# Second layer of a two-layer transformer: the memory attention moved ahead of the differential heads, and projection units issued in halves

## The reference, cut to what matters

```python
h = rmsnorm_2(x, norm_mix[1])
proj = h @ b_w_q                       # q1 | q2 (6 heads of 64 each) | qm (4 memory heads of 64)
q1, q2 = partial_rope(rmsnorm_2(q1)), partial_rope(rmsnorm_2(q2))   # k1, k2, v come from w_kv, likewise
o = diff_attention(q1, q2, k1, k2, v, lam)     # p = softmax(q1 k1) - lam * softmax(q2 k2); o = p v
main = rmsnorm_2(o, b_subln) * (1 - lam_init)  # 6 heads of width 128
mo = memory_attention(qm, mem_n, ...)          # softmax over 256 memory rows, 4 heads
x = x + concat([main, mo]) @ w_o[1]
x = x + sqrelu_mlp(rmsnorm_2(x), w_up[1], w_down[1])
```

## Time and profile before

| | us |
|---|---|
| median of 3 runs | 1125.19 (1123.98 to 1125.64) |
| the profiled execution: its own time | 1122.91 |
| its span, first to last instruction | 1121.1 |
| TensorE matmul busy in the span | 1069.4 |
| VectorE / ScalarE / GpSimd busy | 642.4 / 546.1 / 370.1 |
| mean granted TensorE clock | 0.981 of full |

### The profile page before, as it was taken

How to read it: one execution, slowest core, us unless ns; L and a number is a source line. 1 busy time by engine, 2 the same in 40 slices (tenths; PEclk the granted TensorE clock), 3 DMA queues, 4 the chain that set the end, 5 groups by cost and what they waited for, 6 DMA issues and landing times.

```text
span 1121.1 us, 19839 instructions
## 1 busy us (share of the span) xinstructions
PE 1069.4 (95%) x8566; PEld 1047.2 (93%) x8566; DVE 642.4 (57%) x834; ACT 546.1 (49%) x770; POOL 370.1 (33%) x198
## 2 busy tenths in 40 slices
PE   6889999998999999989999999999999879999998
PEld 6889999998999999989999999999987779999998
DVE  3768855565775554727855444446765546544443
ACT  3367866633556444544344344444554544443341
POOL 2437267130555433352201342231522111252221
PEclk9999999999999999999999999999998889999999
DMA  9987648446387554534456555555532115655541
GB/s 324 285 269 243 209 151 293 159 131 203 94 282 232 188 188 166 173 113 151 135 167 198 180 187 188 186 193 171 169 128 80 39 38 188 218 174 179 182 151 39
DMA packets 173956, 197.39 MB, mean 176 GB/s; under 512 B 5379, under 2 KB 146092, under 8 KB 173740
## 3 DMA queue, kind: packets, MB, share of 16 engines
q1 hardware_dynamic: 173868, 196.11, 54.0%
HBM read 195.03 MB, written 1.06 MB: 175 GB/s over the span
## 4 chain that ended last, share of the span: by engine, by line
PE 83%; DVE 5%; ACT 4%; DMA 2%; POOL 2%; issue 2%; SPq 1%; DVEq 1%; ACTq 0%; POOLq 0%
PE bank L501 82%; DVE w_lo L1709 2%; DMA ada_raw<-in_w_ada 2%; ACT w_hi L1154 1%; SPq L457 1%; ACT ada_raw L1144 1%; POOL ada_raw L1559 1%; DMA probsT<-in_buckets 1%; PE bank L754 0%; DVE fresh L1758 0%; POOL head_bias L1594 0%; DVE big L2120 0%; ACT h_hi L1191 0%; DVE fresh L1752 0%; POOL u_lo L1527 0%
## 5 line engine op out<-in xcount | busy, mean ns | idle before, releaser
L1709 DVE TENSOR_TENSOR w_lo<-w_raw,w_hi 128x2048 fp32r<-128x2048 f32 x158 | 386.9, 2451 | 242.9 <-ACT w_hi L1154 241.6
L501 PE MATMUL bank<-h_hi,w_hi 128*128 128x256 f32 x1328 | 378.3, 290 | 11.9 <-DVE w_lo L1709 7.5
L501 PE MATMUL bank<-h_hi,w_lo 128*128 128x256 f32 x1328 | 373.6, 287 | 0.0
L1154 ACT ACTIVATE w_hi<-w_raw 128x2048 fp32r<-128x2048 f32 x158 | 301.3, 1908 | 131.4 <-PE bank L501 123.8
L501 PE MATMUL bank<-h_lo,w_hi 128*128 128x256 f32 x1328 | 347.5, 284 | 0.6 <-POOL h_lo L1527 0.6
L501 PE MATMUL bank<-u_hi,w_hi 128*128 128x256 f32 x1024 | 287.7, 285 | 4.6 <-ACT u_hi L1163 2.3
L501 PE MATMUL bank<-u_hi,w_lo 128*128 128x256 f32 x1024 | 286.5, 284 | 0.0
L1527 POOL TENSOR_TENSOR u_lo<-fresh,u_hi 128x512 fp32r<-128x512 f32 x60 | 142.3, 2374 | 411.8 <-ACT u_hi L1163 411.6
L501 PEld LDWEIGHTS bank<-h_hi,w_hi 128*128 128x128 f32 x1328 | 259.9, 196 | 17.0 <-DVE w_lo L1709 9.4
L501 PE MATMUL bank<-u_lo,w_hi 128*128 128x256 f32 x1024 | 275.5, 284 | 0.0
L501 PEld LDWEIGHTS bank<-h_hi,w_lo 128*128 128x128 f32 x1328 | 259.6, 196 | 0.0
(11 more groups left out here) (247 smaller groups left out, 1026.2 us busy)
## 6 DMA issues: line engine op xcount, KB each, us to landing
w_raw<-in_w_mlp SPq DMA_DIRECT2D x32, 1024.0 KB, 5.5
w_raw<-in_w_up SPq DMA_DIRECT2D x32, 1024.0 KB, 5.4
w_raw<-in_w_down SPq DMA_DIRECT2D x32, 1024.0 KB, 5.1
w_raw<-in_w_in SPq DMA_DIRECT2D x21, 1024.0 KB, 5.6
ada_raw<-in_w_ada SPq DMA_DIRECT2D x19, 1024.0 KB, 7.8
w_raw<-in_a_w_in SPq DMA_DIRECT2D x10, 1024.0 KB, 5.1
w_raw<-in_w_o SPq DMA_DIRECT2D x8, 1024.0 KB, 4.9
w_raw<-in_w_out SPq DMA_DIRECT2D x4, 1024.0 KB, 4.9
```

Of the source, the lines that this page charges most:

```text
L501: return pe.matmul(dst, lhsT, rhs, start=start, stop=stop, skip_group_check=True)
L1154: act.activation(w_hi[:, n % PARTS_RING, :], w_raw[:, slot_of[n], :], ACT.Copy).then_inc(hi_w, 1)
L1709: dve.tensor_tensor(w_lo[:, n % PARTS_RING, :], w_raw[:, slot_of[n], :], w_hi[:, n % PARTS_RING, :].bitcast(F32), ALU.subtract).then_inc(l ...
```

## The change: what it does

- Unit QM1 moves from sixth to second in the layer (it is unit 113 now). Its scores, turns, `m_pv`, `attended` and `to_T` stand beside units Q0, V0, K1 and Q1, ahead of the first differential head's turn. The pairs use `mem_bank` (`acc[0]`, `acc[1]` for the first, `ps_ada`, `acc[2]` for the second), and `to_T` writes `acc[3]`. New waits: `rotate("k1")` and `d_scores(0)` wait for the copies of the memory's turned probabilities.
- Units K1, Q1, K2, Q2, V1 and V2 are multiplied in halves of 24 matmuls (`half_n`; `half_tok` likewise by token tile), with attention steps between the halves; the unit's evacuation follows the second half. With `product` both output tiles of one weight row stood together.
- The memory's quarter of O1 is the first (`o_part(3, J_YM1, first=True)`), and heads 4 and 5 (quarter 2) the last.
- The programs of ScalarE, VectorE and GpSimd and the list `MISC` follow this order. The number of matmuls, transposes, splits, loads and bytes is the same.

```diff
     heads_unit("k", w["w_kv"], 0)
+    n_unit("qm1", w["b_w_q"][0], MAIN_W, "a")
     heads_unit("q", w["b_w_q"][0], 0)
     n_unit("v", w["w_kv"], MAIN_W, "a")
     heads_unit("k", w["w_kv"], 1)
     heads_unit("q", w["b_w_q"][0], 1)
-    n_unit("qm1", w["b_w_q"][0], MAIN_W, "a")
     heads_unit("k", w["w_kv"], 2)
     heads_unit("q", w["b_w_q"][0], 2)
     n_unit("v", w["w_kv"], MAIN_W + 256, "a")
...
-N_QM0, N_CONV, N_O0, N_M1K, N_MLP1, N_M1V, N_QM1, N_O1, N_MLP2 = 64, 65, 74, 78, 79, 111, 117, 122, 126
-N_K, N_Q, N_V = (112, 115, 118), (113, 116, 119), (114, 120, 121)
+N_QM0, N_CONV, N_O0, N_M1K, N_MLP1, N_M1V, N_QM1, N_O1, N_MLP2 = 64, 65, 74, 78, 79, 111, 113, 122, 126
+N_K, N_Q, N_V = (112, 116, 118), (114, 117, 119), (115, 120, 121)
...
+        mem_bank = [(acc[0], acc[1]), (ps_ada, acc[2])]
...
+                if i == 2:
+                    pe.wait_ge(turned_copied, 2 * (G_M1 + 1) + 2)
...
-            product(N_Q[0], u_hi, u_lo, job=X_MIX1, ready=(x_hi, x_lo))
+            product(N_QM1, u_hi, u_lo, job=X_MIX1, ready=(x_hi, x_lo))
...
+                else:
+                    pe.wait_ge(turned_copied, 2 * G_M1 + 2)
...
+            def half_n(n, nt, hi, lo):
+
+                if nt == 0:
+                    start_unit(n)
+                wh, wl = (t[:, n % PARTS_RING, :].rearrange("p (k n) -> p k n", k=KT) for t in (w_hi, w_lo))
+                for kt in range(KT):
+                    for i, (w, x) in enumerate(((wh, hi), (wh, lo), (wl, hi))):
+                        last = mm(lin[lin_bank[n]][:, nt * T:nt * T + T], w[:, kt, nt * P:nt * P + P], x[:, kt, :],
+                                  nt == 0 and kt == 0 and i == 0, kt == KT - 1 and i == 2)
+                if nt:
+                    last.then_inc(unit_done, 1)
...
             qk_squares("k0", N_K[0])
             rotate("k0", tiles_of("k0"))
+            product(N_Q[0], u_hi, u_lo)
+            qk_squares("qm1", N_QM1)
+            rotate("q0", tiles_of("q0"))
+            m_scores(0)
+            qk_squares("q0", N_Q[0])
             product_tok(N_V[0], h_hi, h_lo)
-            rotate("q0", tiles_of("q0"))
-            qk_squares("q0", N_Q[0])
-            product(N_K[1], h_hi, h_lo)
             spread_qk("k0", acc[3])
-            product(N_Q[1], u_hi, u_lo)
+            pe.wait_ge(rope_read, 2)
+            m_scores(1)
+            half_n(N_K[1], 0, h_hi, h_lo)
+            m_turn(0)
+            half_n(N_K[1], 1, h_hi, h_lo)
+            m_pv(0)
+            d_scores(0)
+            m_turn(1)
             qk_squares("k1", N_K[1])
+            half_n(N_Q[1], 0, u_hi, u_lo)
+            m_pv(1)
             rotate("k1", tiles_of("k1"))
-            d_scores(0)
-            product(N_QM1, u_hi, u_lo)
+            half_n(N_Q[1], 1, u_hi, u_lo)
+            pe.wait_ge(misc_read, misc_no["mem1.1"] + 1)
+            pe.wait_ge(spread_read, spread_no["qk.k0"] + 1)
+            to_T(acc[3:4], y_tok, y_turned)
+            rotate("q1", tiles_of("q1"))
             qk_squares("q1", N_Q[1])
-            rotate("q1", tiles_of("q1"))
-            spread_qk("k1", acc[3])
 
             d_turn(0)
             d_scores(1)
-            product(N_K[2], h_hi, h_lo)
+            half_n(N_K[2], 0, h_hi, h_lo)
             pv(0)
-            qk_squares("qm1", N_QM1)
+            pe.wait_ge(fresh_ready, J_YM1 + 1)
+            spread_qk("k1", acc[3])
+            half_n(N_K[2], 1, h_hi, h_lo)
 
             d_turn(1)
             d_scores(2)
-            product(N_Q[2], u_hi, u_lo)
+            half_n(N_Q[2], 0, u_hi, u_lo)
             pv(1)
             rotate("k2", tiles_of("k2"))
+            half_n(N_Q[2], 1, u_hi, u_lo)
             turn_o(0)
             qk_squares("k2", N_K[2])
 
             d_turn(2)
             d_scores(3)
-            product_tok(N_V[1], h_hi, h_lo)
-            pv(2)
+            half_tok(N_V[1], 0, h_hi, h_lo)
             rotate("q2", tiles_of("q2"))
-            spread_qk("k2", acc[3])
+            half_tok(N_V[1], 1, h_hi, h_lo)
             turn_o(1)
             qk_squares("q2", N_Q[2])
+            spread_qk("k2", acc[3])
+            pv(2)
 
             d_turn(3)
             d_scores(4)
-            pe.wait_ge(spread_read, spread_no["qk.k2"] + 1)
-            m_scores(0)
-            product_tok(N_V[2], h_hi, h_lo)
+            half_tok(N_V[2], 0, h_hi, h_lo)
             pv(3)
+            half_tok(N_V[2], 1, h_hi, h_lo)
+            turn_o(2)
 
             d_turn(4)
             d_scores(5)
-            turn_o(2)
-            m_turn(0)
-            o_part(0, J_DIFF[0], first=True)
+            o_part(3, J_YM1, first=True)
+            turn_o(3)
             pv(4)
-            m_pv(0)
-            m_scores(1)
-            turn_o(3)
+            o_part(0, J_DIFF[0])
 
             d_turn(5)
             pv(5)
             turn_o(4)
-            m_turn(1)
             o_part(1, J_DIFF[1])
-            m_pv(1)
             turn_o(5)
-            pe.wait_ge(misc_read, misc_no["mem1.1"] + 1)
-            pe.wait_ge(d_max, DIFF_HEADS)
-            to_T(acc[0:1], y_tok, y_turned)
             pe.wait_ge(fresh_hi, J_DIFF[2] + 1)
             for m in range(2):
                 part(N_O1 + m, 2, u_hi, u_lo, products="h")
-            pe.wait_ge(fresh_hi, J_YM1 + 1)
+            pe.wait_ge(fresh_lo, J_DIFF[2] + 1)
             for m in range(2):
-                part(N_O1 + m, 3, u_hi, u_lo, products="h")
-            pe.wait_ge(fresh_lo, J_YM1 + 1)
-            for m in range(2):
-                part(N_O1 + m, 2, u_hi, u_lo, products="l")
-                part(N_O1 + m, 3, u_hi, u_lo, last=True, products="l")
+                part(N_O1 + m, 2, u_hi, u_lo, last=True, products="l")
...
             split_w(N_K[0] + AHEAD)
             evac_k(0)
-            split_w(N_Q[0] + AHEAD)
+            split_w(N_QM1 + AHEAD)
             act.wait_ge(lam_dots, 1)
             act.activation(stat[:, S_LAM:S_LAM + 2], stat[:, S_DOT:S_DOT + 2], ACT.Exp).then_inc(lam_exp, 1)
+            evac_qk("qm1", N_QM1, v_tok[:, 0, :], gain=V_MQ + 1)
+            split_w(N_Q[0] + AHEAD)
             evac_q(0)
             split_w(N_V[0] + AHEAD)
+            mem_exps(0)
             evac_v_unit(0)
             split_w(N_K[1] + AHEAD)
+            mem_copy(0)
             evac_k(1)
+            mem_exps(1)
             split_w(N_Q[1] + AHEAD)
+            mem_copy(1)
+            d_exps(0)
             evac_q(1)
-            split_w(N_QM1 + AHEAD)
-            d_exps(0)
-            evac_qk("qm1", N_QM1, v_tok[:, 0, :], gain=V_MQ + 1)
-
+
+            split_w(N_K[2] + AHEAD)
             d_copy(0)
-            split_w(N_K[2] + AHEAD)
             d_exps(1)
             evac_k(2)
 
             d_copy(1)
+            o_square(0)
             split_w(N_Q[2] + AHEAD)
-            o_square(0)
             d_exps(2)
             evac_q(2)
 
             d_copy(2)
+            o_square(1)
+            split_h(J_YM1, u_hi, 6)
             split_w(N_V[1] + AHEAD)
-            o_square(1)
             d_exps(3)
             evac_v_unit(1)
 
             d_copy(3)
+            o_square(2)
             split_w(N_V[2] + AHEAD)
-            o_square(2)
             split_h(J_DIFF[0], u_hi, 0)
             d_exps(4)
-            mem_exps(0)
+            o_square(3)
             evac_v_unit(2)
 
             d_copy(4)
-            o_square(3)
-            copy_turned("mem1.", 0, G_M1, 512, mem_pT)
+            split_w(N_V[2] + AHEAD + 1)
             d_exps(5)
-            split_w(N_V[2] + AHEAD + 1)
+            o_square(4)
 
             d_copy(5)
-            o_square(4)
-            mem_exps(1)
+            split_h(J_DIFF[1], u_hi, 2)
             o_square(5)
-            split_h(J_DIFF[1], u_hi, 2)
-            copy_turned("mem1.", 1, G_M1 + 1, 512, mem_pT)
             split_h(J_DIFF[2], u_hi, 4)
-            split_h(J_YM1, u_hi, 6)
...
             head_unit("k0")
+            power("qk.qm1")
             head_unit("q0")
             head_unit("k1")
             head_unit("q1")
-            power("qk.qm1")
             cos_part("k2", flat(qk, 4, 6))
             o_power(0)
             power("qk.k2")
             cos_part("q2", flat(big, 14, 16))
+            split_h(J_YM1, u_lo, u_hi, 6)
             o_power(1)
             power("qk.q2")
+            o_power(2)
             split_h(J_DIFF[0], u_lo, u_hi, 0)
-            o_power(2)
             o_power(3)
             o_power(4)
+            split_h(J_DIFF[1], u_lo, u_hi, 2)
             o_power(5)
-            split_h(J_DIFF[1], u_lo, u_hi, 2)
             split_h(J_DIFF[2], u_lo, u_hi, 4)
-            split_h(J_YM1, u_lo, u_hi, 6)
             mlp(J_MLP2)
...
-            split_w(N_Q[0] + AHEAD)
+            split_w(N_QM1 + AHEAD)
             dve.wait_ge(misc_read, misc_no["sum6"] + 1)
             head_mean("k0")
             rope_add("k0", k_pair[0])
-            split_w(N_V[0] + AHEAD)
+            split_w(N_Q[0] + AHEAD)
+            head_mean("qm1")
...
+            split_w(N_V[0] + AHEAD)
```

(69 more changed lines are left out.)

21 lines of the change are left out of this document (10 added, 11 removed).

## The result

Over 11 runs each, beside each other on one chip, the kernel before took 1123.98 us (1120.75 to 1126.18) and the changed one **1116.89 us** (1114.13 to 1120.91): ratio 0.994, 95% interval 0.9923 to 0.9956. The forecast was 1113.9 with a range of 1107.5 to 1120.5. Right in sign and range, but of 11.3 us forecast about 7 came. The forecast had started from three runs of the kernel before, with a median of 1125.19 us; over 11 runs it is 1.2 us less, so the forecast time looks closer (3.0 us off) than the forecast gain is (4.2 us off). The profiled execution took 1116.6 us.

A forecast was written before the change was run, and what follows sets the result against it. TensorE bounds the kernel, losing time to hand-over waits and low clock. Floor 106.0 + waits 7.0 + restarts 0.5 + clock 5.4 = 118.9 us against the stage's 130.2: 11.3 less, so 1113.9 from 1125.19; range 1107.5 to 1120.5.

The forecast's parts named there:

- The floor: The stage from Q0 to O1's second unit with no wait and the full clock: 106.0 us of 130.2.
- The memory's move: Memory attention beside Q0 to Q1: its work zero in the sum, the tail's waits around it gained, first head later.
- the walk: Stepping through all four engine programs with profiled durations: d_turn(0) at 840.3, d_turn(5) at 893.0, 11 us behind it.
- The restart of a half: Cost on TensorE of cutting six units in halves: 0 to 1.6 us, taken as 0.5.
- The waits that stay: TensorE's hand-over waits left in the stage by the new order: 7.0 us, at best 3, otherwise up to 13.
- The slower rival: VectorE late at o_scale and o_copy, six heads each paying 3.3 us: 1131.6 us; decides from 2.3 extra per head; chance 0.05.
- the old cadence: Heads paced by their VectorE and ScalarE chain, five still taking 64.5 us: 1123.3; chance 0.12 with waits near upper bound.
- The clock: Two low-clock stretches of 6.8 us, near 874 and 896, costing 2.7 each, 5.4 together; one to three stretches: chance 0.63.
- clock stays up: Waits left too short to lower TensorE's clock, no low stretch in the stage: gain 16.7 us, 1108.5; chance 0.20.

The follow-up runs named there:

- fillers: Extra matmuls read by nobody, put where TensorE waits: 42 on the changed kernel, 1114.29 us; 20 on a later reordered kernel, 1117.2 us.

## Why the prediction was right in sign and range, and where it was off

**The floor held.** 121.3 us less the waits (10.4) and the low clock (4.7, below) is 106.2; the forecast took 106.0, and the other executions agree with it to 1 us.

**The memory's move** was right: `attended` is gone from TensorE's releasers, and no wait in front of `d_turn(0)` is above 0.83. `d_turn(0)` came at 842.59, in a stage that began 2.1 later: 0.2 off the walk. The tail took 11.8 us; the forecast had 11 and, in it, one low stretch worth 2.7. That stretch came before `d_turn(5)` instead, and the 0.8 over 11 is mostly `turn_o(4)`.

**The restart of a half** (0.5 in the sum) cost nothing that the trace shows: a half at full clock takes 2.94 to 2.98 us from its start to that of the next block and a whole unit 5.83 to 5.93. Directly behind `rotate` it is 3.3, and 6.1 for a whole unit before and after.

**The waits that stay**, 7.0 in the sum, measured 10.4: this is the step that failed. Term by term: squares of k2 0.9, measured 1.43; squares of q2 1.1 and 1.19; `pv(4)` with `turn_o(3)` 0.7 and 0.58; `pv(5)` 0.6 and 0.67; `rotate` of q0 and q1 0.9 and 1.3; the high part of the last pair 1.3 and 1.28. These were sized within about 0.1 us, but for the squares of k2 (0.5 short) and `rotate` (0.4 short) (`add_out`'s 0.3 is the 0.4 at 914.0, behind the stage). One of 0.5 for `stat` wasn't foreseen. Two were wrong: `turn_o(2)` was held to be covered (0) and waited 1.53; `turn_o(4)` 1.2 and 1.83. The prediction sized GpSimd's power and VectorE's scale by rows where each ran alone, although already held one operation at 1.43 and the same at 2.71 us, which it used only as a bound for Q0's cosines, and the trace before held the two rows shown above, 2.68 and 1.48 us. The step that failed is therefore "`turn_o(h)` comes a half later, so `o_copy` and `o_scale` are covered". The slower rival described this mechanism (VectorE late at `o_scale` and `o_copy`); it decided at two of six heads, 1.5 and 0.6 over the forecast, and not 2.3 at each. The waits also built up along the heads: against the walk the turns were later by 0.2, 0.3, 0.7, 2.4, 3.8 and 6.7 us, once the stage's start is taken out; the last step holds the second low stretch. `d_turn(5)` at 901.77 is past the 900 that the prediction named as the sign of the old cadence (899.7 once the stage's start is taken out). Five heads took 59.2 us, between the walk's 52.7 and the old 64.5. Of the 6.5 us over the walk, 4.7 are the two low stretches and about 2 the longer waits at `turn_o(2)` and the squares, so it is not that each head keeps its old pace. The other signs, waits of 6 to 8 us in sum and none over 1.5, were missed too; those behind `o_copy` and `o_take` stayed at 6.6, below 10.

**The clock**, 5.4 in the sum, was 4.7 by this execution: half of V1 took 4.5 us instead of 2.9, scores 2.3 instead of 1.5, and O1's first part 5.3 instead of 2.95. That the size agrees is partly luck: the changed kernel's other execution has 13.6 us of low clock in place of 10.2. Two stretches of 6.8 were forecast, near 874 and 896; one of 3.4 and one of 6.8 came at 866.0 and 889.9, each directly behind small blocks with a wait in them. The case "clock stays up" fell, though the longest wait before 866 was 1.43 us, below the 1.75 it took as its measure. No profiled run kept the full clock through the whole stage, those with fillers included. The Trainium skill, "TensorE: Matmul & The Clock Gate", section "Loop structure matters more than you think", has the engine stay warm where matmuls follow a copy out of PSUM at once; in these places TensorE stood waiting for the copy, so the trace does not speak against that rule, only against the 1108.5 that the prediction drew from it.

**Sum:** 3.4 of waits, less 0.5 and 0.7 that came better, is 2.2 of the 2.4 us by which the stage's gain (8.9) missed 11.3; the last 0.2 is the floor. The other 2.6 us between 8.9 and the spans' 6.3 lie outside the stage and are not the change's; by medians the gain is 7.1. How much of those 1.8 us between 7.1 and 8.9 is chance of the profiled execution stays open.

**What stays open.** What sets off a low stretch: one and the same kernel ran from 1109 to 1119 us, and the changed kernel had 10.2 us of low clock in the stage in one profiled execution and 13.6 in another, with nearly the same waits (10.4 and 9.7). No kernel was made to hold its waits fixed and vary the clock alone. And each single edit of VectorE's and GpSimd's order shortened its wait, but its effect on the time is not clear of the noise.

## What to carry to other kernels

Before an operation is moved on VectorE or GpSimd, look at what the other one runs at that moment: in these traces a small operation beside a long one that reads two operands of 128x512 or more could last until after the long one's end, and a move meant to hide it can put it exactly there. Cutting TensorE's work finer can only bring it to its waits sooner, as the halves alone did; look at the order of the engine that answers as well. And where the granted clock steps, compare stage by stage and in several rounds, since a gain of 2 us in waits can drown in the clock elsewhere: the same code ahead of the stage differed by up to 4.9 us between executions.
